# Adding the squares of two features on VectorE before the ones matmul that sums over features

## The chip, the core and the metric

The kernel runs on one core of a Trainium2 chip. TensorE (PE) does matmuls, VectorE (DVE) and ScalarE (ACT) elementwise work, GpSimd (POOL) some of it, SyncE (SP) issues the transfers of weights. Each engine runs its own instructions in order and waits for others by semaphores. The metric is device microseconds (us) of one execution.

## The reference

The program is a first transformer block (sliding-window attention, a recurrence, block attention, a feed-forward part) and then two layers of a second block, for 256 tokens with 1024 features. The change touches only the second block. Each of its layers has four stages, and each stage ends in a projection whose result is normalised before it is added to x:

```python
for l in range(DEPTH_2):                 # 2 layers
    h = rms_norm_2(x, ng[0])
    x = x + 0.5 * rms_norm_2(swiglu(h, w1, w3, w2), ng[1])      # feed-forward
    y = mixer_block(rms_norm_2(x, ng[2]), ...)                  # ends in merged @ w_out
    x = x + rms_norm_2(y, ng[3])
    y = cross_attention(rms_norm_2(x, ng[4]), ...)              # ends in o @ wo
    x = x + rms_norm_2(y, ng[5])
    x = x + 0.5 * rms_norm_2(swiglu(rms_norm_2(x, ng[6]), ...), ng[7])

def rms_norm_2(x, g):
    y = x * rsqrt(mean(x * x, axis=-1) + RMS_EPS)
    return y * g
```

The mean of x * x runs over the 1024 features. All is f32.

## The kernel before, in words

**Layout.** Features lie on the 128 partitions, in eight feature tiles (f = 0 to 7), and tokens on the free axis, so a feature tile is 128x256. A sum over features is therefore a sum over partitions and over the eight tiles: TensorE does it with a 128x128 matrix of ones, which adds up a tile and leaves the sum on every partition, and the eight tiles accumulate in one PSUM region (STAT, a part of misc_ps).

**Matmuls.** Weights come from memory in units of up to four k tiles by 256 columns (SP). ScalarE rounds a unit to weights_hi (`hi`, L1099), VectorE takes the rest weights_lo = weights - weights_hi (`lo`, L1421), and TensorE does three fp32r matmuls for each tile (L842). There are four buffers of split weights: at the step of unit m, ScalarE and VectorE split unit m + 3 (AHEAD = 3). The rounding of unit m + 3 waits until unit m - 1 has been multiplied, which frees its buffer. A GEMM over 256 output columns (two feature tiles, a pair) has six units in w2 of the feed-forward stages (22 k tiles: five units of four and one of two), and two units in the output projections of the mixer and of the cross-attention.

**Order.** `plan` writes one list of steps, and each engine runs through that list and does its own part of every step, in that order. For VectorE the step of unit m is the split of unit m + 3.

**The end of a stage.** Four GEMMs c = 0 to 3 give the four pairs of y. For each pair ScalarE writes the squares of two feature tiles to SQ (squares, L1181) and then y times the gain (L1184). Step `ystat` (L917) sums a pair's squares on TensorE: two fp32 matmuls by ones (L922). An fp32 matmul stands in the trace as two instructions, so a pair is four of them. The `ystat` of pair c - 1 stands behind GEMM c in the list, that of pair 3 follows that of pair 2:

```python
for c in range(4):
    gemm("w2", c * COLS, 22, ("HID", key), "evac_y", ft=2 * c, sq=s, yk=key, ...)
    if c:
        add("ystat", s=s, c=c - 1)
add("ystat", s=s, c=3)
add("rstd", key=key + "y", s=s, out="RY")
```

Then ScalarE takes the logarithm (L1103) and the exponential (L1105) of the sum, each with a load of its table before it, and VectorE multiplies y by the result (L1574) and adds it to x (L1576). In the mixer stage more lies in between: behind GEMM 1 the memory is transposed (L1062) and copied (L1903), behind GEMM 2 it is split (L1555) and squared, and after the `ystat` of pair 3 its own statistic is summed (L913), into the same PSUM region, once the logarithm has read it.

There are eight such stages (four feed-forward, two mixer, two cross-attention), so 32 `ystat` steps.

Of the kernel before, what the change touches and what calls it, by code (L numbers as in the profile page):

```python
# [19 lines left out]
ALU = mybir.AluOpType  # L20
# [4 lines left out]
T = 256  # L25
TT = T // P
D = 1024
NF = D // P
# [527 lines left out]
def build(nc, a, out, scratch, marks, final, stop=None):  # L556
# [10 lines left out]
    SQ = sb("squares", [P, NF, T])  # L567
# [8 lines left out]
    ONES, IDENT, FLIP, HEADS = (sb(n, [P, P]) for n in ("ones", "ident", "flip", "headsum"))  # L576
# [48 lines left out]
    STAT = PB[:, 3, :]  # L625
# [9 lines left out]
    sems = {n: ctx.enter_context(nc.semaphore(n)) for n in names}  # L635
# [4 lines left out]
    def up(name, reached=None, by=1):  # L640

        count[name] = count.get(name, 0) + by
        if reached is not None:
            marks[reached] = (name, count[name])
        return count[name]
# [4 lines left out]
    def at(*reached):  # L650

        assert reached in marks or not final, reached
        return marks.get(reached, (None, 1))[1]
# [161 lines left out]
    def _(pe):  # L815
        state = dict(att=None, scores=None)

        def stat_free(s):
            if stat_before.get(s) is not None:
                pe.wait_ge(*done(("stat_read", stat_before[s])))  # L820
# [96 lines left out]
        def pe_ystat(k):  # L917
            if k["c"] == 0:
                stat_free(k["s"])
            pe.wait_ge(sems["act_drain"], at("sqy", k["s"], k["c"]))  # L920
            for f in (2 * k["c"], 2 * k["c"] + 1):
                mm = pe.matmul(STAT[:, 0:T], ONES[:], SQ[:, f, :], start=f == 0, stop=f == NF - 1)  # L922
            mm.then_inc(sems["pe_norm"], 1)
            up("pe_norm", ("stat", k["s"]) if k["c"] == 3 else None)

# [141 lines left out]
        def pe_finish(k):  # L1067
# [3 lines left out]
            for t in range(TT):  # L1071
                for f in range(NF):
                    mm = pe.transpose(GPF[:, t * D + f * P:t * D + (f + 1) * P], X[:, f, t * P:(t + 1) * P], IDENT[:])
            mm.then_inc(sems["pe_setup"], 1)
            up("pe_setup", ("out_ps",))

        parts = dict(unit=pe_unit, params=pe_params, turn_x=pe_turn_x, mod=pe_mod, mod_col=pe_mod_col, bias=pe_bias, stat=pe_stat, ystat=pe_ystat,
                     rstd_cols=pe_rstd_cols, qk_norm=pe_qk_norm, scores=pe_scores, turn=pe_turn, pv=pe_pv,
                     subln=pe_subln, rnn_gate=pe_rnn_gate, cln_mean=pe_cln_mean, cln_var=pe_cln_var,
# [334 lines left out]
    def _(dve):  # L1414
# [147 lines left out]
        def vec_residual(k):  # L1562
# [14 lines left out]
                                     op0=ALU.mult, op1=ALU.add).then_inc(sems["vec_norm"], 1)  # L1577
            up("vec_norm", ("x", k["v"], p))

        def vec_rstd_cols(k):  # L1580
            dve.wait_ge(sems["pe_norm"], at("rt_ps", k["s"]))
            dve.tensor_copy(RT[:], STAT.rearrange("p (t q) -> p t q", q=P)[:, 0:TT, 0]).then_inc(sems["vec_norm"], 1)
            dve.wait_ge(sems["vec_norm"], up("vec_norm", ("stat_read", k["s"])))
# [316 lines left out]
        def vec_mem_turn(k):  # L1900
            for half in range(2):
# [2 lines left out]
                up("vec_norm", ("memf", f"l{k['l']}", half))  # L1904

        parts = dict(setup=vec_setup, params=vec_params, turn_x=vec_turn_x, mod=vec_mod, mod_sum=vec_mod_sum, adapt=vec_adapt, split=vec_split,
                     residual=vec_residual, rstd_cols=vec_rstd_cols, evac_qk=vec_evac_qk, qk_norm=vec_qk_norm,
                     evac_scaled=vec_scaled, evac_v2=vec_v2, softmax=vec_softmax, pv=vec_pv, subln=vec_subln,
                     pads1=vec_pads1, pads_f1=vec_pads_f1, rnn_conv=vec_rnn_conv, rnn_in=vec_rnn_in, rnn_mult=vec_rnn_mult, evac_yr=vec_evac_yr, gelu=vec_gelu, conv31=vec_conv31, rnn_scan=vec_rnn_scan,
                     evac_gate=vec_evac_gate, evac_branch=vec_evac_branch, evac_ffn_gate=vec_ffn_gate,  # L1910
# [167 lines left out]
```

## Time and profile before

| what | us |
|---|---|
| median of 3 runs | 2551.26 (2547.99 to 2553.19) |
| the profiled execution | 2549.33 |
| its span, first to last instruction | 2547.5 |
| busy: PE / DVE / ACT / POOL | 2365.3 / 1721.2 / 1323.8 / 387.5 |
| share of the chain that ended last: PE / DVE / ACT | 75% / 15% / 6% |

Busy time is the time in which an engine executes something; the chain of waits shows which of it the end depended on. Matmuls overlap: a record of 0.28 us is followed by the next after about 0.12 us, so paces are read from the chain or from start to start.

### The profile page before, as it was taken

The page shows a single profiled execution, that of the slowest core. Times are in us where ns is not written, and L with a number is a line of the kernel's source. Part 1 is how long each engine was busy: PE and PEld are TensorE (multiplying, and loading weights), DVE is VectorE, ACT ScalarE, POOL GpSimd, SP SyncE. Part 2 cuts the span into 40 slices and gives each one's busy share as a digit, 9 for nine tenths or more (in the row PEclk, how much of TensorE's full clock was granted, in tenths as well). Part 3 has the DMA queues.
Part 4 walks back from the last instruction along what each step waited for, and adds up shares of the span by engine and source line. Part 5 has one row for each costly group of instructions (what it writes and reads, how often), then busy time and mean ns, then how long its engine had stood idle before and what let it go on. Part 6 is the DMA issues. An engine that isn't in the chain of part 4 may idle for free.

```text
span 2547.5 us, 44221 instructions
## 1 busy us (share of the span) xinstructions
PE 2365.3 (93%) x18041; PEld 2265.1 (89%) x18041; DVE 1721.2 (68%) x2425; ACT 1323.8 (52%) x2074; POOL 387.5 (15%) x354
## 2 busy tenths in 40 slices
PE   6998998999998998999898998999998999898997
PEld 5976898999998997889898998998987889898997
DVE  5666886886664897887555654664897887555663
ACT  2565445664444654665635445444654765635443
POOL 1000000110110564530000110110464530000110
PEclk9998999999999998999999999999998999999998
DMA  8534584566655462446344654655462345344652
GB/s 246 161 108 141 169 252 140 184 193 211 187 179 158 147 185 83 124 133 195 120 133 125 183 183 140 182 173 175 133 199 75 120 135 182 132 139 120 184 175 82
DMA packets 402041, 400.41 MB, mean 157 GB/s; under 512 B 18006, under 2 KB 399304, under 8 KB 401841
## 3 DMA queue, kind: packets, MB, share of 16 engines
q1 hardware_dynamic: 399457, 389.27, 50.2%
q0 software_dynamic: 2384, 8.32, 1.2%
q8 instruction: 144, 2.36, 0.4%
q14 instruction: 56, 0.46, 0.1%
HBM read 396.45 MB, written 1.09 MB: 156 GB/s over the span
## 4 chain that ended last, share of the span: by engine, by line
PE 75%; DVE 15%; ACT 6%; issue 4%; DMA 1%; ACTq 0%; POOL 0%; DVEq 0%; POOLq 0%
PE gemm_ps L842 62%; DVE weights_lo L1421 4%; PE gemm_ps L845 3%; DVE y L1857 3%; PE misc_ps L970 2%; PE misc_ps L969 2%; PE misc_ps L913 2%; ACT L1103 1%; ACT weights_hi L1099 1%; DVE y L1574 1%; DVE x_res L1576 1%; DVE mod_partial L1518 1%; ACT h_hi L1170 1%; PE misc_ps L1002 1%; ACT e L1218 1%
## 5 line engine op out<-in xcount | busy, mean ns | idle before, releaser
L1421 DVE TENSOR_TENSOR weights_lo<-raw_weights,weights_hi 128x1024 fp32r<-128x1024 f32 x704 | 859.2, 1230 | 467.0 <-ACT weights_hi L1099 463.5
L842 PE MATMUL gemm_ps<-h_hi,weights_hi 128*128 128x256 f32 x3664 | 1068.0, 291 | 68.1 <-DVE h_lo L1555 45.4
L1099 ACT CAST weights_hi<-raw_weights 128x1024 fp32r<-128x1024 f32 x704 | 718.6, 1031 | 664.2 <-PE gemm_ps L842 612.0
L842 PE MATMUL gemm_ps<-h_lo,weights_hi 128*128 128x256 f32 x3664 | 1049.0, 286 | 0.0
L842 PE MATMUL gemm_ps<-h_hi,weights_lo 128*128 128x256 f32 x3664 | 1048.6, 286 | 0.0
L842 PEld LDWEIGHTS gemm_ps<-h_hi,weights_hi 128*128 128x128 f32 x3664 | 716.2, 195 | 81.5 <-issue 68.0
L842 PEld LDWEIGHTS gemm_ps<-h_lo,weights_hi 128*128 128x128 f32 x3664 | 716.7, 196 | 4.0 <-issue 3.0
L842 PEld LDWEIGHTS gemm_ps<-h_hi,weights_lo 128*128 128x128 f32 x3664 | 715.5, 195 | 0.0
L1986 POOL TENSOR_TENSOR y<-y,prod 128x256 f32<-128x256 f32 x240 | 249.3, 1039 | 352.4 <-ACT prod L1359 197.0
L1974 POOL TENSOR_TENSOR hidl<-hf,hidh 128x512 fp32r<-128x512 f32 x55 | 73.4, 1334 | 1291.1 <-ACT hidh L1343 1291.1
L842 PE MATMUL gemm_ps<-hidh,weights_hi 128*128 128x256 f32 x880 | 248.0, 282 | 0.3 <-DVE weights_lo L1421 0.3
L842 PE MATMUL gemm_ps<-hidh,weights_lo 128*128 128x256 f32 x880 | 245.4, 279 | 0.0
L842 PE MATMUL gemm_ps<-hidl,weights_hi 128*128 128x256 f32 x880 | 245.4, 279 | 0.0
L1857 DVE SCALAR_TENSOR_TENSOR y<-zp,param_cols,y 128x256 f32<-128x256 f32 x240 | 187.2, 780 | 5.7
L842 PE MATMUL gemm_ps<-gh,weights_hi 128*128 128x256 f32 x544 | 160.9, 296 | 18.4 <-DVE gl L1558 14.7
L842 PEld LDWEIGHTS gemm_ps<-hidh,weights_hi 128*128 128x128 f32 x880 | 165.2, 188 | 0.7 <-DVE weights_lo L1421 0.5
L842 PEld LDWEIGHTS gemm_ps<-hidh,weights_lo 128*128 128x128 f32 x880 | 165.4, 188 | 0.0
L842 PEld LDWEIGHTS gemm_ps<-hidl,weights_hi 128*128 128x128 f32 x880 | 164.7, 187 | 0.2
L842 PE MATMUL gemm_ps<-gl,weights_hi 128*128 128x256 f32 x544 | 154.7, 284 | 0.0
L842 PE MATMUL gemm_ps<-gh,weights_lo 128*128 128x256 f32 x544 | 154.4, 284 | 0.0
L842 PEld LDWEIGHTS gemm_ps<-gh,weights_hi 128*128 128x128 f32 x544 | 105.3, 194 | 22.1 <-issue 20.3
L1359 ACT ACTIVATE prod<-zp,param_cols 128x256 f32<-128x256 f32 x240 | 104.8, 505 | 3.2 <-POOL y L1986 3.2
(282 smaller groups left out, 2833.2 us busy)
## 6 DMA issues: line engine op xcount, KB each, us to landing
raw_weights<-in_ffn_w_dram SPq DMA_DIRECT2D x256, 512.0 KB, 3.8
raw_weights<-in_w_in_dram SPq DMA_DIRECT2D x200, 512.0 KB, 3.7
raw_weights<-in_w_mod_dram SPq DMA_DIRECT2D x48, 512.0 KB, 4.9
raw_weights<-in_w_up_dram SPq DMA_DIRECT2D x44, 512.0 KB, 4.5
raw_weights<-in_xattn_kv_dram SPq DMA_DIRECT2D x32, 512.0 KB, 3.8
raw_weights<-in_w_out_dram SPq DMA_DIRECT2D x24, 512.0 KB, 3.9
raw_weights<-in_w_down_dram SPq DMA_DIRECT2D x20, 512.0 KB, 4.7
raw_weights<-in_w_branch_dram SPq DMA_DIRECT2D x16, 512.0 KB, 4.4
```

Of the source, the lines that this page charges most:

```text
L842: mm = pe.matmul(ps[:, c, 0:T], w[:, m, kt, c * P:(c + 1) * P], x[:, f, :], start=start, stop=stop_)
L845: mm = pe.matmul(ps[:, c, 0:u["cols"]], x[:, f, c * P:(c + 1) * P], w[:, m, kt, 0:u["cols"]], start=start, stop=stop_)
L913: mm = pe.matmul(STAT[:, 0:T], ONES[:], squares[:, f, :], start=f == 0, stop=f == NF - 1)
L969: pe.matmul(ps, c["q"][m][:, qt * P:(qt + 1) * P], c["k"][m][:, 0:nk], start=True, stop=False)
L970: mm = pe.matmul(ps, FLIP[:], c["hank"][:, c["head"][m], T - nk:T], start=False, stop=True)
L1002: mm = pe.matmul(PV[:, f * T:(f + 1) * T], c["v"][f][kb], PT[:, kb * T:(kb + 1) * T], start=kb == 0, stop=kb == 1)
L1099: act.copy(WH[s], RAWB[:, u["raw"] % RAW, 0:u["nkt"], 0:u["cols"]]).then_inc(sems["weights_rounded"], 1)
L1359: act.activation(o_m["prod"][:, b, i, :], o_m["zp"][:, f, j:j + T], ACT.Copy, scale=col(f"dw{k['l']}", 8 * j + f)).then_inc(sems["act_prod ...
L1421: dve.tensor_tensor(WL[s], RAWB[:, u["raw"] % RAW, 0:u["nkt"], 0:u["cols"]], WH[s], ALU.subtract).then_inc(sems["weights_rest"], 1)
L1857: dve.scalar_tensor_tensor(out=Y[:, f, :], in0=o_m["zp"][:, f, j:j + T], scalar=col(f"dw{l}", 8 * j + f), in1=Y[:, f, :], op0=ALU.mult, op ...
L1974: pool.tensor_tensor(l_[:, s, :], src, h[:, s, :], ALU.subtract).then_inc(sems["hidden_rest"], 1)
L1986: pool.tensor_tensor(Y[:, f, :], Y[:, f, :], o_m["prod"][:, b, i, :], ALU.add).then_inc(sems["pool_conv"], 1)
```

## The change

The `ystat` step gets a part on VectorE: it waits for ScalarE's squares of the pair and adds the second feature tile to the first, in place. TensorE waits for that addition in place of the squares and does one ones matmul instead of two. Nothing else is edited.

```diff
         def pe_ystat(k):
             if k["c"] == 0:
                 stat_free(k["s"])
-            pe.wait_ge(sems["act_drain"], at("sqy", k["s"], k["c"]))
-            for f in (2 * k["c"], 2 * k["c"] + 1):
-                mm = pe.matmul(STAT[:, 0:T], ONES[:], SQ[:, f, :], start=f == 0, stop=f == NF - 1)
+            pe.wait_ge(sems["vec_norm"], at("sqy_sum", k["s"], k["c"]))
+            mm = pe.matmul(STAT[:, 0:T], ONES[:], SQ[:, 2 * k["c"], :], start=k["c"] == 0, stop=k["c"] == 3)
             mm.then_inc(sems["pe_norm"], 1)
             up("pe_norm", ("stat", k["s"]) if k["c"] == 3 else None)
...
+        def vec_ystat(k):
+            f = 2 * k["c"]
+            dve.wait_ge(sems["act_drain"], at("sqy", k["s"], k["c"]))
+            dve.tensor_tensor(SQ[:, f, :], SQ[:, f, :], SQ[:, f + 1, :], ALU.add).then_inc(sems["vec_norm"], 1)
+            up("vec_norm", ("sqy_sum", k["s"], k["c"]))
...
-                     residual=vec_residual, rstd_cols=vec_rstd_cols, evac_qk=vec_evac_qk, qk_norm=vec_qk_norm,
+                     residual=vec_residual, ystat=vec_ystat, rstd_cols=vec_rstd_cols, evac_qk=vec_evac_qk, qk_norm=vec_qk_norm,
```

VectorE's order at the end of the first feed-forward stage before, from the splits of w2's first units on (L1421 is the split of a unit, L1574 the first instruction of the residual; a unit of two k tiles is 128x512):

```order
532 L1421 TENSOR_TENSOR weights_lo<-raw_weights,weights_hi 128x512
533 L1421 TENSOR_TENSOR weights_lo<-raw_weights,weights_hi 128x1024 x5
534 L1421 TENSOR_TENSOR weights_lo<-raw_weights,weights_hi 128x512
535 L1421 TENSOR_TENSOR weights_lo<-raw_weights,weights_hi 128x1024 x5
536 L1421 TENSOR_TENSOR weights_lo<-raw_weights,weights_hi 128x512
537 L1421 TENSOR_TENSOR weights_lo<-raw_weights,weights_hi 128x1024 x5
538 L1421 TENSOR_TENSOR weights_lo<-raw_weights,weights_hi 128x512
539 L1421 TENSOR_TENSOR weights_lo<-raw_weights,weights_hi 128x1024 x3
540 L1574 TENSOR_TENSOR y<-y,rstd_y 128x512
```

And the same place in the changed kernel, where the addition is L1582 and the split L1420:

```order
532 L1420 TENSOR_TENSOR weights_lo<-raw_weights,weights_hi 128x512
533 L1420 TENSOR_TENSOR weights_lo<-raw_weights,weights_hi 128x1024 x5
534 L1420 TENSOR_TENSOR weights_lo<-raw_weights,weights_hi 128x512
535 L1420 TENSOR_TENSOR weights_lo<-raw_weights,weights_hi 128x1024 x3
536 L1582 TENSOR_TENSOR squares<-squares 128x256
537 L1420 TENSOR_TENSOR weights_lo<-raw_weights,weights_hi 128x1024 x2
538 L1420 TENSOR_TENSOR weights_lo<-raw_weights,weights_hi 128x512
539 L1420 TENSOR_TENSOR weights_lo<-raw_weights,weights_hi 128x1024 x3
540 L1582 TENSOR_TENSOR squares<-squares 128x256
541 L1420 TENSOR_TENSOR weights_lo<-raw_weights,weights_hi 128x1024 x2
542 L1420 TENSOR_TENSOR weights_lo<-raw_weights,weights_hi 128x512
543 L1420 TENSOR_TENSOR weights_lo<-raw_weights,weights_hi 128x1024 x3
```

The addition of pair c - 1 stands behind the split of the third unit of GEMM c + 1, three units ahead of the unit that TensorE multiplies last before it comes to the same step. The additions of pairs 2 and 3 follow behind row 543.

At the end of the mixer stage VectorE has this in the changed kernel (ml is the lower part of the split memory, memf its copy):

```order
821 L1420 TENSOR_TENSOR weights_lo<-raw_weights,weights_hi 128x1024 x4
822 L1582 TENSOR_TENSOR squares<-squares 128x256
823 L1908 COPY memf<-misc_ps 128x1024 x2
824 L1420 TENSOR_TENSOR weights_lo<-raw_weights,weights_hi 128x1024 x2
825 L1582 TENSOR_TENSOR squares<-squares 128x256
826 L1554 SCALAR_TENSOR_TENSOR ml<-memf,param_cols,mh 128x256 x8
827 L1420 TENSOR_TENSOR weights_lo<-raw_weights,weights_hi 128x1024 x2
828 L1582 TENSOR_TENSOR squares<-squares 128x256 x2
829 L1573 TENSOR_TENSOR y<-y,rstd_y 128x512
```

Before, the same rows stand there without the three rows of L1582: the last two additions come behind eight parts of the memory's split and two weight splits.

On TensorE nothing changes its place; one ones matmul is left of two. Before, behind GEMM 1 of the first feed-forward stage:

```order
5086 L842 MATMUL gemm_ps<-hidh,weights_lo 128x256
5087 L922 MATMUL misc_ps<-squares,ones 128x256 x2
5088 L842 MATMUL gemm_ps<-hidh,weights_hi 128x256
```

## Rows read from the trace of the kernel before

**Rows 1.** The page, busy time, share of the span and instructions.
```profile
PE 2365.3 (93%) x18041; PEld 2265.1 (89%) x18041; DVE 1721.2 (68%) x2425; ACT 1323.8 (52%) x2074; POOL 387.5 (15%) x354
```

**Rows 2.** Chain of waits, 778 to 836 us: start, length, engine, line.
```profile
781.57 0.86 PE misc_ps L922 x4
782.43 15.55 PE gemm_ps L842 x132
797.98 0.86 PE misc_ps L922 x4
798.84 15.56 PE gemm_ps L842 x132
...
829.73 0.50 DVE h_lo L1555
830.22 0.04 issue
```

**Rows 3.** Timeline, 795 to 801 us: start, length, engine, instruction [idle before].
```profile
797.70 0.74 PEld L922 LDWEIGHTS misc_ps<-squares,ones 128*128 128x128 f32 x4
797.74 1.22 DVE L1421 TENSOR_TENSOR weights_lo<-raw_weights,weights_hi 128x1024 fp32r<-128x1024 f32 x1 [1.60 <-ACT weights_hi L1099]
797.82 1.03 PE L922 MATMUL misc_ps<-squares,ones 128*128 128x256 f32 x4
```

**Rows 4.** Groups of instructions by form: count, busy us, mean ns, idle before.
```profile
L1555 DVE SCALAR_TENSOR_TENSOR h_lo<-pu,h_hi 128x256 fp32r<-128x256 f32 x16 | 5.5, 417 | 0.0
...
L1738 DVE TENSOR_TENSOR xc<-xc,s_all 128x256 f32<-128x256 f32 x8 | 3.4, 425 | 0.3
```

**Rows 5.** Timeline, projections of a mixer and a cross stage.
```profile
1199.94 2.77 DVE L1555 SCALAR_TENSOR_TENSOR h_lo<-pu,h_hi 128x256 fp32r<-128x256 f32 x8
...
1210.54 1.22 DVE L1421 TENSOR_TENSOR weights_lo<-raw_weights,weights_hi 128x1024 fp32r<-128x1024 f32 x1 [0.49 <-ACT weights_hi L1099]
...
1211.97 0.74 PEld L922 LDWEIGHTS misc_ps<-squares,ones 128*128 128x128 f32 x4
...
1346.16 1.23 DVE L1421 TENSOR_TENSOR weights_lo<-raw_weights,weights_hi 128x1024 fp32r<-128x1024 f32 x1 [0.49 <-ACT weights_hi L1099]
...
1347.59 0.74 PEld L922 LDWEIGHTS misc_ps<-squares,ones 128*128 128x128 f32 x4
```

**Rows 6.** Chain of waits behind the mixer's third projection.
```profile
1222.18 0.60 ACT squares L1181
```

**Rows 7.** Timeline, the end of a feed-forward stage.
```profile
814.15 1.23 DVE L1421 TENSOR_TENSOR weights_lo<-raw_weights,weights_hi 128x1024 fp32r<-128x1024 f32 x1 [1.60 <-ACT weights_hi L1099]
...
815.77 1.28 ACT L1103 ACT_TABLE_LOAD   x1
817.07 0.47 ACT L1103 ACTIVATE rstd_y<-misc_ps,eps 128x256 f32<-128x256 f32 x1
```

**Rows 8.** Timeline, the ends of a mixer and a cross stage.
```profile
1229.75 2.36 DVE L1421 TENSOR_TENSOR weights_lo<-raw_weights,weights_hi 128x1024 fp32r<-128x1024 f32 x2 [2.53 <-ACT weights_hi L1099]
...
1233.19 0.47 ACT L1103 ACTIVATE rstd_y<-misc_ps,eps 128x256 f32<-128x256 f32 x1
...
1233.72 5.41 PE L913 MATMUL misc_ps<-msq,ones 128*128 128x256 f32 x16 [1.38 <-ACT rstd_y L1103]
...
1361.14 0.60 ACT L1181 ACTIVATE squares<-gemm_ps 128x512 f32<-128x512 f32 x1 [1.78 <-PE gemm_ps L842]
...
1363.78 0.47 ACT L1103 ACTIVATE rstd_y<-misc_ps,eps 128x256 f32<-128x256 f32 x1
```

**Rows 9.** Timeline of TensorE, two matmuls behind idle time.
```profile
145.28 1.22 PE L939 MATMUL misc_ps<-small_squares,headsum 128*128 128x512 f32 x1 [1.54 <-ACT rg L1272]
...
1200.50 0.36 PE L842 MATMUL gemm_ps<-h_hi,weights_hi 128*128 128x256 f32 x1 [1.94 <-DVE h_lo L1555]
```

**Rows 10.** Busy by stretch: PE, PEld, DVE, ACT, POOL, granted clock, DMA share, GB/s.
```profile
145.00:146.00 1.00, 0.71 (x1) 0.50 (x2) 0.00 (x0) 1.00 (x2) 0.00 (x0) 0.62 0.85 251
1200.00:1201.00 1.00, 0.50 (x4) 0.53 (x5) 1.00 (x5) 0.94 (x3) 0.00 (x0) 1.00 0.97 325
```

## The prediction

> **What bounds the kernel now.** I read the page first: TensorE (PE) is busy 93% of the span [rows 1]. Which instruction on it matters is not in that share, so the second view was the chain of waits around one output projection of a feed-forward stage [rows 2]. The reader is to see there 132 matmuls of a projection (15.55 us), 0.86 us of L922 (the ones matmuls of the change), and again 132 matmuls: nothing but TensorE, back to back, and L922 stands on the path as itself. An ones matmul is recorded as two instructions, so four of them for a pair of features cost 0.86 us, or 0.43 us a matmul. The third view was the timeline around one such place, for what VectorE (DVE) does at that moment [rows 3]. The fourth was the same for the ends of stages, where TensorE waits for others [rows 7, 8].
>
> **Where the 32 places are.** Eight stages (four feed-forward, two mixer, two cross-attention) have four output projections c = 0 to 3 each. The program puts the sum of pair c-1 behind projection c, and the sums of pairs 2 and 3 both behind projection 3. So per stage two sums stand between projections (pairs 0 and 1) and two at its end. 64 ones matmuls become 32.
>
> **What is removed.** One matmul of 0.43 us in each place. Of the 32, the 16 between projections can be on the path; the 16 at the ends stand beside ScalarE's (ACT) evacuation and table load.
>
> **What is added, feed-forward stages.** Each sum now waits for an addition on VectorE, and VectorE runs in program order. The order listing shows what is ahead of the addition: the split of weights (L1421) for the third unit after the one that TensorE is in. Why that is late: the split waits for ScalarE's rounding, and that waits for the end of TensorE's unit before. In w2 a projection has 22 k tiles, five units of four and a last one of two. The last is 12 of 132 matmuls, 15.55 x 12 / 132 = 1.41 us; the split takes 1.22 [rows 3] and the rounding comes before it. In the rows [rows 3]: TensorE starts L922 at 797.70 (its weight load), VectorE begins the split only at 797.74 and ends it at 798.96. Then comes the addition. 128x256 f32 TENSOR_TENSOR takes 0.425 us (L1738) [rows 4]. Consecutive VectorE instructions with no dependence overlap a little: eight of 0.417 us [rows 4] took 2.77 us [rows 5], one each 0.34 us, so a record overlaps the one before by about 0.08. The addition ends at 798.96 - 0.08 + 0.42 = 799.30. From a VectorE end to TensorE: the chain has h_lo, 0.04 us of issue and then a matmul [rows 2]; I take 0.05. TensorE starts the sum at 799.35 instead of 797.70: +1.65 us; one matmul less: -0.43; net +1.22. With the overlap left out it is +1.30; I take 1.25 for all eight places (four stages, pairs 0 and 1), whose chain pieces repeat: 8 x 1.25 = **+10.0 us**. Nothing gives that back: VectorE and ScalarE get ahead by the same time, but in that stretch they wait for TensorE (the split's own row has 1.60 us of waiting before it [rows 3]), and the next projection is 15.55 us of TensorE again. Behind the addition on VectorE waits the next split, which waits for ScalarE anyway as this one does, so it is not later.
>
> **Mixer and cross stages.** Here a projection is two full units of 24 matmuls, so split and unit end together. Mixer: VectorE ends its split at 1210.54 + 1.22 = 1211.76, TensorE loads for L922 at 1211.97 [rows 5]. Addition to 1212.10, release 1212.15: +0.18 - 0.43 = -0.25. Cross: 1346.16 + 1.23 = 1347.39, to 1347.73, release 1347.78 against 1347.59: +0.19 - 0.43 = -0.24 [rows 5]. The mixer's pair 1 counts nothing: behind it the chain leaves TensorE for ScalarE at 1222.18 [rows 6] and stays there until the end of the stage. That leaves pair 0 in two mixers and both pairs in two cross stages: 6 x -0.24 = **-1.4 us**.
>
> **Ends of stages.** Feed-forward: VectorE's split ends at 814.15 + 1.23 = 815.38, two additions to 815.72 and 816.06, TensorE from 815.77, both sums in the 0.12 + 1.03 us that four such instructions take from the first weight load [rows 3], so until 816.92. The logarithm of L1103 starts at 817.07, held by a table load that began at 815.77 and takes 1.28 us [rows 7]. Cost nothing, with 0.15 us to spare; if that cover were gone it would be up to 0.7 us in each. Cross: squares end at 1361.74, addition to 1362.2, sum to about 1363.0, logarithm at 1363.78 [rows 8]: nothing. Mixer: VectorE is late with two splits, 1229.75 + 2.36 = 1232.11 [rows 8]; additions to 1232.45 and 1232.79, TensorE 1232.50 to 1233.65, logarithm at 1233.69 instead of 1233.19: +0.50 us. The statistic of the memory (L913) waits for that read at 1233.72, so it is on the path. Two mixers: **+1.0 us**.
>
> **Sum.** +10.0 - 1.4 + 1.0 = +9.6 us. The profiled execution took 2549.33 us (span 2547.5), so 2558.9 by its own time. It lies 1.9 us under the median of the runs, 2551.26; from the median it is 2560.9. I say 2561.
>
> **What the trace doesn't show.** An idle gap of about 1.65 us inside dense matmuls, eight times. For the granted clock after it there are rows on both sides [rows 9, 10]: after 1.94 us of idle time at 1200.50 the stretch has clock 1.00 (2.4 GHz); after 1.54 us at 145.28 the clock was 0.62 in that microsecond, part of it at 1.2 GHz. What a fall costs: L913 took 5.41 us for 16 instructions at 1233.72 [rows 8] where 4 take 0.86 [rows 2], that is 3.44, so 1.97 us lost. Bounds for eight gaps: 0 and 8 x 1.97 = 15.8 us. I take 0, since the longer of the two gaps, which like these lies before feature matmuls of a projection, kept its clock, and keep the other end for the range. The addition itself is bounded by 0.34 us (the overlapped pace) and 0.425 without overlap: at most 0.1 us a place, 1 us in all.
>
> **A rule to weigh.** The profile's busiest engine is TensorE, and it loses work in this change [rows 1]. The Trainium skill ("Perfetto Trace Analysis", Identifying the Most-Contended Engine) says to optimise the engine with the highest occupancy first, though it warns that matmul busy time misleads. By that rule the change is a gain, 16 x 0.43 = 6.9 us on the path. The trace speaks against it: what counts is who releases the sum, and that becomes the split and the addition.
>
> **Rivals.**
> 1. Forecast, stalls at the feed-forward projections: +9.6, 2561, own range 2557 to 2564. 67%.
> 2. The clock falls in a part of the gaps, two to eight of them at 1.5 to 2 us: 2564 to 2576. For it: the row at 145.28, and the gap of 1.38 us before L913. Against it: the row at 1200.50. 16%.
> 3. The other side, faster: the sums are released in time and only the removed matmuls count, -6.9 us, 2544. Its place is the same as mine, pairs 0 and 1 between projections; it decides if the addition ends before TensorE has finished its unit, 1.65 us earlier than I work out. For it: chain row L922 and 0.43 us each [rows 2]. Against it: the order of the splits. 4%.
> 4. Stalls are there but absorbed, within 5 us of before: if the units behind waited for something else than TensorE. Against it: the chain holds TensorE alone [rows 2]. About 2553. 9%.
> 5. The ends cost too (feed-forward ends, 0.15 us of cover): three or four more times 0.3 to 0.7 us: 2563. 4%.
>
> This kernel can tell 0.2% (5.1 us) from no change. Faster by more: 5% (case 3 and a little of 4). Within: 11%. Slower: 84%. The range 2555 to 2570 leaves out case 3, half of case 4 and the worst of case 2.
>
> **What would show it.** In the profile after: VectorE has 32 new instructions of about 0.42 us; the first two of each feed-forward stage start as a split ends. TensorE is idle about 1.6 us before the sum there, eight times, released by VectorE. In cross stages the gap is 0.2 us. Ones matmuls of the sums: 64 instructions in place of 128. The stretch from one projection to the next in feed-forward stages goes from 16.41 us (15.55 + 0.86) to about 17.66. Granted clock 1.00 across these gaps confirms case 1 over 2. The forecast is wrong if the gaps are absent, or present with no longer span.

## The result: 11.5 us slower, and the profile after

| | before | after |
|---|---|---|
| median (6 runs each) | 2552.23 us (2547.89 to 2557.76) | 2563.75 us (2562.29 to 2564.89) |
| ratio, 95% interval | | 1.0045 [1.0031, 1.0059] |
| profiled execution / its span | 2549.33 / 2547.5 us | 2563.45 / 2561.6 us |
| granted clock, mean | 0.966 | 0.958 |

The forecast was 2561 us, +9.6. The page after, busy time, answers to [rows 1]:

```profile
PE 2357.3 (92%) x17977; PEld 2256.9 (88%) x17977; DVE 1732.2 (68%) x2457; ACT 1323.9 (52%) x2074; POOL 388.3 (15%) x354
```

TensorE has 64 instructions and 8 us of work less, VectorE 32 instructions and 11 us more, and the whole takes longer. Where, the chain of waits around the first feed-forward stage says (start, length, engine, line; the split is L1420 now, the ones matmul L921, the addition L1582; PEld below is TensorE's loading of weights). It answers to [rows 2]:

```profile
780.93 1.06 ACT weights_hi L1098
...
782.02 1.23 DVE weights_lo L1420
...
783.24 0.34 DVE squares L1582
783.59 0.14 issue
783.72 0.67 PE misc_ps L921 x2
784.39 15.56 PE gemm_ps L842 x132
...
801.32 0.70 PE misc_ps L921 x2
802.02 15.57 PE gemm_ps L842 x132
```

Before, this stretch held TensorE alone. Now, at the first place, it leaves TensorE for a rounding on ScalarE, the split on VectorE and the addition behind it. (At the second place the view follows ScalarE's evacuation instead; see below.) From one projection's first matmul to the next one's it is 802.02 - 784.39 = 17.63 us; before it was 16.41, and 17.66 was forecast. The timeline at the second of these places (idle time before an instruction in brackets) answers to [rows 3]:

```profile
799.70 1.23 DVE L1420 TENSOR_TENSOR weights_lo<-raw_weights,weights_hi 128x1024 fp32r<-128x1024 f32 x1 [1.60 <-ACT weights_hi L1098]
...
800.85 0.42 DVE L1582 TENSOR_TENSOR squares<-squares 128x256 f32<-128x256 f32 x1
...
801.32 0.30 PEld L921 LDWEIGHTS misc_ps<-squares,ones 128*128 128x128 f32 x2 [1.58 <-DVE squares L1582]
801.32 0.70 PE L921 MATMUL misc_ps<-squares,ones 128*128 128x256 f32 x2 [1.38 <-ACT y L1183]
```

The addition begins 1.15 us behind the start of the split, overlapping its end by 0.08, and TensorE begins 0.05 us after the addition's end. The weight load waited 1.58 us. (For the matmul the view names ScalarE's evacuation, y, which ends within 0.04 us of the addition. The program has TensorE wait for the addition alone, and in e5 below the ones matmul at the first place starts at 783.48 while y runs until 783.71. So y is not what it waits for.)

The ends of stages, answering to [rows 7, 8], are these in the timeline: feed-forward, mixer, and the last ones matmul of a cross stage.

```profile
818.48 0.75 DVE L1582 TENSOR_TENSOR squares<-squares 128x256 f32<-128x256 f32 x2
818.95 0.73 PEld L921 LDWEIGHTS misc_ps<-squares,ones 128*128 128x128 f32 x4 [1.58 <-DVE squares L1582]
818.95 1.13 PE L921 MATMUL misc_ps<-squares,ones 128*128 128x256 f32 x4 [1.38 <-DVE squares L1582]
818.95 1.28 ACT L1102 ACT_TABLE_LOAD   x1
820.25 0.47 ACT L1102 ACTIVATE rstd_y<-misc_ps,eps 128x256 f32<-128x256 f32 x1
...
1235.14 2.36 DVE L1420 TENSOR_TENSOR weights_lo<-raw_weights,weights_hi 128x1024 fp32r<-128x1024 f32 x2 [2.53 <-ACT weights_hi L1098]
...
1237.41 0.75 DVE L1582 TENSOR_TENSOR squares<-squares 128x256 f32<-128x256 f32 x2
...
1237.89 1.13 PE L921 MATMUL misc_ps<-squares,ones 128*128 128x256 f32 x4 [3.99 <-DVE squares L1582]
1239.06 0.47 ACT L1102 ACTIVATE rstd_y<-misc_ps,eps 128x256 f32<-128x256 f32 x1 [0.49 <-PE misc_ps L921]
...
1366.76 0.70 PE L921 MATMUL misc_ps<-squares,ones 128*128 128x256 f32 x2 [0.54 <-DVE squares L1582]
```

In the feed-forward stage the sums end at 820.08 and the logarithm starts at 820.25, when its table is loaded: hidden, as forecast. In the mixer stage the logarithm waits 0.49 us for the sum: the +0.50 of the forecast, at this instruction. Whether it reaches the end of the kernel is another matter, and is taken up at the end.

**How the stages are compared.** ScalarE's squares of a stage's four pairs are four marks on each trace. From the first to the fourth lie projections 1 to 3 and the sums of pairs 0 and 1, nothing else. Before, in the first feed-forward stage: 766.05 to 814.43, 48.38 us; after, 766.74 to 817.61, 50.87: +2.49, for two places. From the fourth mark to the logarithm is the stage's end. This is what each kernel shows against before (mean of its stages, us; "sum" is all eight stages and the mixer ends; the last column is the ratio of its runs to runs of the kernel before taken beside them on the same chip. The chips differ between experiments, so the ratios compare, not the medians):

| kernel | feed-forward (x4) | mixer (x2) | cross (x2) | mixer end (x2) | sum | ratio [interval] |
|---|---|---|---|---|---|---|
| after | +2.49 | -0.20 | -0.47 | +0.48 | +9.6 | 1.0045 [1.0031, 1.0059] |
| e2 | +2.48 | 0 | 0 | 0 | +9.9 | 1.0037 [1.0024, 1.0051] |
| e3 | 0 | -0.20 | -0.47 | +1.42 | +1.5 | 0.9995 [0.9987, 1.0004] |
| e4 | +3.34 | 0 | 0 | 0 | +13.4 | 1.0050 [1.0037, 1.0063] |
| e5 | +1.87 | -0.43 | -0.87 | +1.15 | +7.2 | 1.0032 [1.0020, 1.0043] |
| e6 | -0.88 | -0.43 | -0.87 | 0 | -6.1 | 0.9983 [0.9974, 0.9992] |
| e1 | -0.88 | -0.44 | -0.87 | +0.91 | -4.3 | 0.9988 [0.9979, 0.9996] |
| e7 | -0.88 | -0.44 | -0.87 | +0.56 | -5.0 | 0.9988 [0.9977, 0.9998] |
| e8 | -1.74 | -0.86 | -1.71 | +2.36 | -7.4 | 0.9983 [0.9974, 0.9993] |
| e9 | +7.30 | -0.20 | -0.47 | +1.42 | +30.7 | 1.0133 [1.0119, 1.0147] |
| e10 | -1.74 | -0.51 | -1.71 | +0.07 | -11.3 | 0.9964 [0.9950, 0.9978] |

0.001 of the ratio is 2.5 us. Several of these kernels compute something else than the program (their expectations say what they leave out or count twice); they are there for their time alone.

In the cuts of code, what stands behind a `#` is a note.

### The profile page after: what moved, and what is told of

Its sections match the earlier page's. It is cut to its first block, busy times and chain, and to the rows that moved or that the text cites. A ratio compares the mean times of both kernels' runs of the same rounds, so it can differ in the third digit from the quotient of the medians.

```text
span 2561.6 us, 44125 instructions
## 1 busy us (share of the span) xinstructions
PE 2357.3 (92%) x17977; PEld 2256.9 (88%) x17977; DVE 1732.2 (68%) x2457; ACT 1323.9 (52%) x2074; POOL 388.3 (15%) x354
## 3 DMA queue, kind: packets, MB, share of 16 engines
q8 instruction: 144, 2.36, 0.4%
## 4 chain that ended last, share of the span: by engine, by line
PE 75%; DVE 15%; ACT 6%; issue 3%; DMA 1%; ACTq 0%; POOL 0%; DVEq 0%; POOLq 0%
PE gemm_ps L842 62%; DVE weights_lo L1420 4%; PE gemm_ps L845 3%; DVE y L1862 3%; PE misc_ps L969 2%; PE misc_ps L968 2%; PE misc_ps L913 2%; ACT weights_hi L1098 1%; DVE y L1573 1%; ACT L1102 1%; DVE x_res L1575 1%; DVE mod_partial L1517 1%; ACT h_hi L1169 1%; PE misc_ps L1001 1%; ACT e L1217 1%
## 5 line engine op out<-in xcount | busy, mean ns | idle before, releaser
L1420 DVE TENSOR_TENSOR weights_lo<-raw_weights,weights_hi 128x1024 fp32r<-128x1024 f32 x704 | 859.5, 1231 | 474.6 <-ACT weights_hi L1098 470.8
L842 PEld LDWEIGHTS gemm_ps<-gl,weights_hi 128*128 128x128 f32 x544 | 106.0, 195 | 1.2 <-issue 1.0
```

What stands on the lines that cost most here:

```text
L842: mm = pe.matmul(ps[:, c, 0:T], w[:, m, kt, c * P:(c + 1) * P], x[:, f, :], start=start, stop=stop_)
L1420: dve.tensor_tensor(WL[s], RAWB[:, u["raw"] % RAW, 0:u["nkt"], 0:u["cols"]], WH[s], ALU.subtract).then_inc(sems["weights_rest"], 1)
```

## The experiments

### e2 and e3: the two halves of the change

In e2 only the feed-forward places of pairs 0 and 1 have the addition, all others two matmuls as before; e3 is the complement.

```diff
+def FOLD(k):
+    return k.get("ffn", False) and k["c"] < 2      # e3: not (...)
...
+            if FOLD(k):
                 pe.wait_ge(sems["vec_norm"], at("sqy_sum", k["s"], k["c"]))
                 mm = pe.matmul(STAT[:, 0:T], ONES[:], SQ[:, 2 * k["c"], :], ...)
+            else:
+                pe.wait_ge(sems["act_drain"], at("sqy", k["s"], k["c"]))
+                for f in (2 * k["c"], 2 * k["c"] + 1):
...
         def vec_ystat(k):
+            if not FOLD(k):
+                return
```

> The change is made only for pairs 0 and 1 of the four feed-forward stages (8 of 32 places); elsewhere the sum is as before. My theory (the addition stands behind a late weight split, so TensorE waits about 1.6 us before each of these sums and saves 0.43): +1.2 us a place as the profile after shows, +9.6 to 10.0 us over before, ratio about 1.0038, which is nearly all of the change's cost. Rival 'the cost lies at the stage ends': within 2 us of before. Rival 'the clock falls after the gaps': more than +12 us, with granted clock under 1 in the stretch behind them.

> The complement: the change everywhere but in those 8 places. My theory: -1.4 us between the projections of the mixer and cross stages, +1.0 us at the two mixer ends, so -0.4 us, the same as before within the noise. Rival 'the cost lies at the stage ends': +5 to +10 us.

Measured: e2 2563.90 us, ratio 1.0037, that is 9.4 us with an interval of 6 to 13; e3 2551.01 us, ratio 0.9995. Eight places of 32 carry the cost; the other 24 together are within what can be told from nothing. The rows of e2 and e3 in the table are those of the changed kernel, split in two, but for one: the mixer end of e3 costs 1.42 instead of 0.48 us. Its timeline of TensorE (the ones matmul is L926 here, the sum of the memory's squares L917):

```profile
1231.34 2.08 PE L926 MATMUL misc_ps<-squares,ones 128*128 128x256 f32 x4 [4.00 <-DVE squares L1593]
1233.98 6.70 PE L917 MATMUL misc_ps<-msq,ones 128*128 128x256 f32 x16 [0.56 <-ACT rstd_y L1111]
```

The same four instructions took 1.13 us in the changed kernel, behind the same idle 3.99 us. The missing 0.95 us is the clock, not the wait. Windows over the four instructions, in e3 and in the changed kernel (the column before the last two is the granted clock):

```profile
1231.30:1233.40 2.10, 2.06 (x4) 1.18 (x4) 0.32 (x1) 0.71 (x1) 0.00 (x0) 0.50 0.89 261
...
1237.80:1239.00 1.20, 1.11 (x4) 0.67 (x4) 0.37 (x2) 0.76 (x1) 0.00 (x0) 0.98 0.96 313
```

### e6 and e5: no addition; then only the wait

e6 does one ones matmul for each pair with no addition (VectorE's part of the step is never called; the squares of the odd feature tiles are left out of the sum). e5 is e6 with TensorE waiting, for pairs 0 to 2, until the split ahead of which the addition would stand is done.

```diff
-            pe.wait_ge(sems["vec_norm"], at("sqy_sum", k["s"], k["c"]))
+            pe.wait_ge(sems["act_drain"], at("sqy", k["s"], k["c"]))
+            if k["c"] < 3 and state["m"] + AHEAD < len(splits):                     # e5 alone
+                pe.wait_ge(sems["weights_rest"], at("rest", state["m"] + AHEAD))    # e5 alone
             mm = pe.matmul(STAT[:, 0:T], ONES[:], SQ[:, 2 * k["c"], :], ...)
```

> One ones matmul a pair and no addition at all (the squares of the odd feature tiles are left out of the sum), TensorE waits for ScalarE's squares as before. This bounds what the removed matmuls can be worth. My theory: only those between projections on the path count, 14 x 0.43 = -6.0 us against before. Rival 'every TensorE instruction removed shortens the run, since it is the busiest engine': 32 x 0.43 = -13.8 us.

> One ones matmul a pair, no addition; for pairs 0, 1 and 2 TensorE waits for the weight split behind which the addition stood (the squares of the odd feature tiles are left out). It parts the wait into split and addition. My theory: the split alone makes 1.31 us of the delay in a feed-forward place, net +0.88, 8 x 0.88 = +7.0; in mixer and cross the split is done in time, 6 x -0.43 = -2.6; sum about +4.5 us over before. Rival 'the addition on VectorE is what costs': -6 us, like the run without an addition.

Measured: e6 2549.00 us, ratio 0.9983; e5 2557.55 us, ratio 1.0032. The chain of e6:

```profile
781.62 0.43 PE misc_ps L921 x2
782.05 15.54 PE gemm_ps L842 x132
797.60 0.43 PE misc_ps L921 x2
```

So a ones matmul on the path is worth 0.44 us (0.88 for two places), as forecast, and taking them away does make the kernel faster. In e5 the wait for the split alone turns -0.44 into +0.94 a place: 1.38 of the 1.68 us that the wait costs is the split; the rest, 1.24 - 0.94 = 0.30, is the addition. The expectation missed one thing, the mixer ends: they cost 1.15 us each, and with them the sum is +7.2, where the ratio stands for 8 and +4.5 was expected. TensorE waits there for two late splits, and its four instructions then run at half clock (granted clock 0.50 in 1236.70:1238.90):

```profile
1236.79 2.05 PE L924 MATMUL misc_ps<-squares,ones 128*128 128x256 f32 x4 [3.93 <-DVE weights_lo L1423]
```

Of the 1.15 us, 2.05 - 1.13 = 0.92 is the clock again.

### e4: the wait with nothing removed

Feed-forward places of pairs 0 and 1 only: the addition and the wait as in the change, and still two matmuls.

```diff
             if FOLD(k):
                 pe.wait_ge(sems["vec_norm"], at("sqy_sum", k["s"], k["c"]))
-                mm = pe.matmul(STAT[:, 0:T], ONES[:], SQ[:, 2 * k["c"], :], ...)
+                for f in (2 * k["c"], 2 * k["c"] + 1):
+                    mm = pe.matmul(STAT[:, 0:T], ONES[:], SQ[:, f, :], ...)
```

> Only in pairs 0 and 1 of the feed-forward stages: TensorE waits for VectorE's addition, but still does both ones matmuls (the sum then counts one feature tile twice). The price of the wait alone. My theory: 8 x 1.65 = +13.2 us over before, 0.43 us a place more than the run with one matmul there. Rival 'the matmul saved is worth nothing, since TensorE idles there anyway': the same time as with one matmul, +9.6 us.

Measured: 2562.67 us, ratio 1.0050. 3.34 us for two places is 1.67 for one; the prediction's bare wait was 1.65. It and the matmul add up: 1.67 - 0.44 = 1.23, the changed kernel has 1.24.

### e1: the addition ahead of the split

The addition of pairs 0 to 2 is issued on VectorE just ahead of the split behind which it stood; all else is as in the change.

```diff
+        early, last = {}, None
+        for i, (kind, k) in enumerate(steps):
+            if kind == "unit":
+                last = i
+            elif kind == "ystat" and k["c"] < 3:
+                early[last] = k
+        for i, (kind, k) in enumerate(steps):
+            if i in early:
+                vec_ystat(early[i])
...
-            if kind in parts:
+            if kind in parts and not (kind == "ystat" and k["c"] < 3):
```

> The change with one move: on VectorE the addition of pairs 0, 1 and 2 stands ahead of the split that is issued with the last unit of the next projection, not behind it. My theory: it is then done long before TensorE comes to the sum, the waits are gone and the removed matmul counts: 14 places x -0.43 = -6.0 us, and +0.9 us at the two mixer ends, so about -5 us against before (2547) and -16 us against the change. Rival 'it is the addition or its semaphore as such, not its place': no better than the change, about +10 us.

Measured: 2547.77 us, ratio 0.9988. The same 32 additions and the same matmuls, one place earlier on one engine, and the feed-forward stages go from +2.49 to -0.88, the same as with no addition at all. The mixer ends cost 0.91 us each where 0.9 was expected for both together; the clock makes half of it (granted 0.50 in 1232:1236, where two instructions of L921 took 1.22 us; in e7, at full clock, 0.70). The timeline:

```profile
796.30 0.42 DVE L1582 TENSOR_TENSOR squares<-squares 128x256 f32<-128x256 f32 x1
...
797.95 0.30 PEld L921 LDWEIGHTS misc_ps<-squares,ones 128*128 128x128 f32 x2
797.99 1.23 DVE L1420 TENSOR_TENSOR weights_lo<-raw_weights,weights_hi 128x1024 fp32r<-128x1024 f32 x1 [1.27 <-ACT weights_hi L1098]
```

The addition is done 1.23 us before TensorE loads the ones.

### e7: the addition on GpSimd

```diff
-            dve.wait_ge(sems["act_drain"], at("sqy", k["s"], k["c"]))
-            dve.tensor_tensor(SQ[:, f, :], SQ[:, f, :], SQ[:, f + 1, :], ALU.add).then_inc(sems["vec_norm"], 1)
+            pool.wait_ge(sems["act_drain"], at("sqy", k["s"], k["c"]))
+            pool.tensor_tensor(SQ[:, f, :], SQ[:, f, :], SQ[:, f + 1, :], ALU.add).then_inc(sems["pool_sum"], 1)
```

> The changed kernel with all 32 additions on GpSimd in place of VectorE (a semaphore of their own, the ones matmul waits for it). Theory (the cost in the feed-forward places is that VectorE's addition stands behind the split that waits for ScalarE's rounding, not the addition itself): GpSimd has nothing in its queue there, so the addition starts when the squares are written; it takes some 1 us on GpSimd (its 128x256 additions take 1042 ns each in the trace of before), which still ends before the last matmuls of the next projection. All places then gain what one matmul is worth: in-stage growth like the kernel without an addition, feed-forward -0.88, mixer -0.43, cross -0.87 a stage, ratio about 0.998; at the stage ends the slower addition may cost 0.6 in each of the eight, so 0.998 to 1.000. Rival (the addition itself or its semaphore is what costs, on whatever engine): feed-forward +2 or more a stage, ratio 1.004.

Measured: 2546.92 us, ratio 0.9988. The additions take a median of 857 ns there, twice VectorE's, and cost nothing between the projections: the feed-forward stages show -0.88 again. The rival, that the addition or its semaphore is what costs on whatever engine, falls. Timeline:

```profile
797.24 0.87 POOL L2022 TENSOR_TENSOR squares<-squares 128x256 f32<-128x256 f32 x1 [15.11 <-ACT squares L1180]
```

### e9: a longer gap

Three more additions in a row in the eight feed-forward places, to see whether the clock falls behind a longer gap.

```diff
+            if k.get("ffn") and k["c"] < 2:
+                for i in range(3):
+                    dve.wait_ge(sems["vec_norm"], count["vec_norm"])
+                    dve.tensor_tensor(SQ[:, f, :], SQ[:, f, :], SQ[:, f + 1, :], ALU.add).then_inc(sems["vec_norm"], 1)
...
```

> The change with three further additions in series in each of the 8 feed-forward places (the pair's second tile is counted four times), so the gaps grow by 3 x 0.43 us to about 2.7 us. It tells whether the price of a gap is its length or also the clock behind it. My theory: linear, 8 x 1.3 = +10.4 us over the change, +22 over before, granted clock 1.00 behind the gaps. Rival 'the clock falls behind such gaps': up to 2 us more in each, +12 to +26 over the change, with matmul records of 0.41 us behind the gaps.

Measured: 2584.59 us, ratio 1.0133. The timeline of TensorE at the first two of the eight places and the next to last:

```profile
783.70 0.67 PE L921 MATMUL misc_ps<-squares,ones 128*128 128x256 f32 x2 [2.85 <-DVE squares L1587]
...
802.68 0.75 PE L921 MATMUL misc_ps<-squares,ones 128*128 128x256 f32 x2 [2.76 <-DVE squares L1587]
...
2520.61 1.19 PE L921 MATMUL misc_ps<-squares,ones 128*128 128x256 f32 x2 [2.85 <-DVE squares L1587]
```

And the two microseconds behind the first two (busy time of PE, PEld, DVE, ACT, POOL, then the granted clock):

```profile
784.40:786.40 2.00, 2.00 (x19) 2.00 (x18) 0.29 (x1) 0.00 (x0) 0.00 (x0) 1.00 0.34 95
803.50:805.50 2.00, 2.00 (x11) 2.00 (x11) 0.26 (x1) 0.00 (x0) 0.00 (x0) 0.50 0.36 99
```

Behind six of the eight gaps the clock is at 0.50 (1.2 GHz), behind two of 2.85 us it stays full. The theory of a linear price falls, and its rival holds. The three additions cost 1.38 us at a place without a fall (17.69 us from one pair's squares to the next in the changed kernel, 19.06 here, at the first place of the first stage), so a stage would be 2.49 + 2 x 1.38 = +5.25; the four show +6.26, 6.72, 8.24 and 7.97 with one, one, two and two falls. A fall cost 1.0 to 1.5 us. The eight gaps of the changed kernel, 1.38 to 1.47 us on TensorE's matmuls, all kept the clock. Two of the eight windows:

```profile
785.80:787.80 2.00, 2.00 (x20) 2.00 (x19) 0.01 (x1) 0.49 (x1) 0.00 (x0) 1.00 0.45 151
803.50:805.50 2.00, 2.00 (x19) 2.00 (x18) 0.00 (x0) 0.56 (x1) 0.00 (x0) 1.00 0.51 148
```

### e8 and e10: towards a faster kernel

If a sum between projections can be had for nothing, none is needed there. In e8 VectorE adds each pair into pair 0 (128x512), ahead of the split as in e1, and TensorE does two ones matmuls at the stage's end.

```diff
         def pe_ystat(k):
+            if k["c"] < 3:
+                return
+            stat_free(k["s"])
+            pe.wait_ge(sems["vec_norm"], at("sqy_sum", k["s"], 3))
+            for f in (0, 1):
+                mm = pe.matmul(STAT[:, 0:T], ONES[:], SQ[:, f, :], start=f == 0, stop=f == 1)
...
         def vec_ystat(k):
...
+            s = slice(2 * k["c"], 2 * k["c"] + 2)
...
+            dve.tensor_tensor(SQ[:, 0:2, :], SQ[:, 0:2, :], SQ[:, s, :], ALU.add).then_inc(sems["vec_norm"], 1)
```

> VectorE adds the squares of pairs 1, 2 and 3 into pair 0 (three additions of 128x512 a stage, pairs 1 and 2 ahead of the split as in the run before), and TensorE does two ones matmuls a stage, at its end, in place of eight. My theory: nothing is left between projections, 14 places x -0.86 = -12.0 us against before, and at the ends two matmuls behind an addition of 0.69 us: nothing in feed-forward and cross, +0.8 us in the mixers (two): -10.4 us, 2541. Rival 'the longer addition at the end is exposed': 0.5 us or more in each of eight ends, -6 us.

Measured: 2547.88 us, ratio 0.9983, so 4.3 us faster where 10.4 was expected. Between projections it gains twice what e1 does (-1.74 a feed-forward stage), but each mixer end gives 2.36 us back, where 0.4 was expected (0.93 of it is the clock, as the last line below shows), and three of the four feed-forward ends 0.20. At the mixer end the chain shows why (e8; the addition is L1588):

```profile
1229.97 1.11 issue
1231.08 0.68 DVE squares L1588
1231.76 0.06 DVE weights_lo L1422
1231.82 0.99 issue
1232.81 0.69 DVE squares L1588
1233.51 0.14 issue
1233.64 2.06 PE misc_ps L923 x4
```

Two additions, each behind a split, are in series, and the four instructions behind them ran at the lowered clock (2.06 us, not 1.13). e10 takes both away: pairs 1 and 2 are added with the evacuation of their own projection, and pair 3 is not added but gets its own two matmuls.

```diff
+            pe.wait_ge(sems["vec_norm"], at("sqy_sum", k["s"], 2))
+            for f in (0, 1):
+                pe.matmul(STAT[:, 0:T], ONES[:], SQ[:, f, :], start=f == 0, stop=False)
+            pe.wait_ge(sems["act_drain"], at("sqy", k["s"], 3))
+            for f in (6, 7):
+                mm = pe.matmul(STAT[:, 0:T], ONES[:], SQ[:, f, :], start=False, stop=f == 7)
...
+            if kind == "evac_y" and k["sq"] is not None and k["ft"] in (2, 4):
+                vec_ystat(dict(s=k["sq"], c=k["ft"] // 2))
```

> A version meant to be faster: VectorE adds pair 1 and pair 2 into pair 0 (two additions of 128x512 a stage), each issued with the evacuation of its own projection and so ahead of the next splits; pair 3 is not added. TensorE does four ones matmuls at the end of a stage (two of the accumulated pair, two of pair 3), none between the projections. Theory: between the projections two whole gaps of matmuls go, in-stage -1.74 feed-forward, -0.86 mixer, -1.71 cross as in the kernel that accumulates all four pairs, sum -12.1; the ends stand as before (that kernel gave 3.0 back at each mixer end, where its last two additions stood behind splits, and some 1.2 at each feed-forward end). So about -9 to -12, ratio 0.9955 to 0.9965. Rival (what a stage end or a memory transfer behind it gives back is given back whatever the cause): ratio 0.998 as in the kernel that accumulates four.

Measured: 2540.03 us, ratio 0.9964 [0.9950, 0.9978], 5.6 to 12.7 us faster than before. The expected range was met, with two shifts inside it: a mixer stage gains 0.50 us and not 0.86, since the first addition (0.69 us) now stands ahead of the memory's copy on the chain, and the first mixer end still costs 0.12 us, the second nothing. Chain of waits of e10 up to the end of the first feed-forward stage:

```profile
772.95 38.41 PE gemm_ps L842 x326
811.36 0.02 issue
811.38 0.60 ACT squares L1185
```

Where the chain of before had projections with ones matmuls between them [rows 2], and that of after had five pieces on three engines, 326 matmuls now follow one another.

### e11: the changed kernel a second time

> The changed kernel again, unaltered, for a second profile. Theory (the 2.4 to 2.9 us that its first profile shows from the last squares of two feed-forward stages to the mixer stage behind, in stretches that the change doesn't touch, come with the place at which the granted clock falls, not with the change): in-stage growth again +2.48 a feed-forward stage, -0.20 mixer, -0.47 cross to within 0.05, but the stretches between the stages differ from the first profile by up to 3 us, and stretches of lowered clock stand at other places. Rival (the change has a further cost there): the same +2.4 and +2.9 again.

Measured, one execution: 2561.86 us, span 2560.1. The stages show +2.48, -0.20 and -0.47 again. From the last squares of the first feed-forward stage to the first of the mixer stage it is +1.79 us against before, +2.41 in the first profile; at the same stretch of layer 2 it is +2.89 and +2.90. Two profiles of one kernel decide little: one number repeats and one does not.

The other kernels say more. None edits that stretch, and in them it differs from before by -1.6 to +3.4 us: -1.24 and +2.79 within e10 alone, +0.30 and -1.61 in e4, +1.85 and +3.43 in e6, which has no added wait at all. So these microseconds come and go without the change. What they go with is the granted clock. In layer 2 the stretch takes 389.4 us at a mean granted clock of 0.969 (e4), 391.0 at 0.965 (before, e3), 390.6 at 0.961 (e1, e5, e7), 391.9 and 392.8 at 0.956 and 0.957 (e9, e2), 393.8 to 393.9 at 0.952 (both profiles of the changed kernel, e8, e10) and 394.5 at 0.944 (e6). Layer 1 has nearly the same order (390.9 us at 0.965, 394.5 and 394.8 at 0.948), with e5 off it by 2 us. Why one profile has more stretches of lowered clock there than another stays open.

## Why the prediction was right, step by step

**Who releases the sum.** Forecast: the split, then the addition. The chain after has just these at the first place, and at the second the weight load names the addition. e1 and e7 take the addition from behind the split in two ways and both reach e6's number to 0.01 us.

**Feed-forward places, 8 x 1.25.** Measured 1.24. The parts: bare wait 1.67 (e4; forecast 1.65), matmul 0.44 (e6; forecast 0.43), overlap of a VectorE record with the one before 0.08 (forecast 0.08). This came out because each part had a row; only the release at the first place of a stage took 0.14 us (783.58 to 783.72) where 0.05 was written, so that place is +1.28 and the second +1.21.

**Mixer and cross, 6 x -0.24.** Measured -0.20 a mixer stage (one place) and -0.47 a cross stage (two): -1.3 in all against -1.4.

**Ends.** Forecast +0.50 at a mixer end, 0 elsewhere; measured +0.48 at the logarithm, and 0.00 at the six others (2.64 us from squares to logarithm in both kernels). Rival 5 is out. But the forecast also took these 2 x 0.5 us to reach the end of the kernel, and that is not shown. From the last squares of a mixer stage to the first of the cross stage it was 111.60 us in both layers before; it is 111.18 and 111.59 after, 111.56 and 111.77 in the second profile, all at a mean granted clock of 0.969. What offsets the later logarithm is open. In the first layer the statistic of the memory (L913) ran almost wholly at the lowered clock (6.77 us, 5.41 before), and a later part of the stretch at the full clock: before, the next four L913 instructions took 2.05 us on the chain, after 1.13. Where the clock falls moves more here than the 0.48 us in question.

**Clock.** Forecast: no fall in the eight gaps. None fell. e9 shows that the rival was real and its size about right: 1.0 to 1.5 us a fall where 1.5 to 2 was written. Here luck has a part: the forecast took the side of one of two rows that spoke against each other, and neither told why it should hold; with gaps of 2.8 us that choice would have missed 8.2 us (what the four stages of e9 show beyond 5.25 each).

**The sum.** +9.6 against a measured ratio that stands for 8 to 15 us, and against +14.1 in the two profiled spans. The stages with the mixer ends hold 9.6 of the 14.1, 8.6 of it between the first and the fourth squares of stages; 5.3 lie in the two unedited stretches of e11's section, +0.7 ahead of the first stage, and -1.5 in the rest, nearly all of it directly behind the two mixer ends, as just told. So what is shown part by part is the 8.6 between projections. That the whole came within 3 us of the forecast owes something to parts that it did not have and that happened to be small in sum. The prediction compares two single executions as if unedited stretches were equal; they are so to about 3 us each. It had no term for that; the range covered it.

**A slip that changed nothing.** Rival 3 and the rule count 16 x 0.43 = 6.9 us as the most that the removed matmuls can give. By the forecast's own reading the mixer's pair 1 is not on the path, so it is 14 x 0.43 = 6.0; e6's stages show 6.1.

**The rule.** The Trainium skill ("Perfetto Trace Analysis", Identifying the Most-Contended Engine) says to optimise the engine with the highest occupancy first. Read as "work taken from it pays", which is the prediction's reading, it fails in this case: TensorE's busy time fell by 8 us and the kernel lost 11. e6 shows the condition under which it holds: the same work taken away with no new wait gains 4 us.

## What to carry to other kernels

Moving work from the busiest engine to one with time to spare pays only if the second engine gets to it in time. What decides is not its busy share (68%) but what stands ahead of the new instruction in its program order, and what that waits for. Here the same addition cost 10 us behind a split, and nothing between the projections ahead of it. At the mixer ends, where the last addition still stands behind two splits, it cost 0.9 us, half of it the clock. Once an off-path engine does such an addition ahead of its slow step, fold further: one sum at the end in place of four (e10). Where the last additions stand behind splits again, the end of the stage takes a part of it back (e8).

## What the runs showed of the hardware

The same idle time can be followed by either clock level. Ahead of the mixer's projections TensorE was idle 1.94 us in the kernel before and kept the full clock [rows 9, 10]; in the changed kernel the same place shows matmuls of 0.42 us behind 1.93 us idle. Timeline and window:

```profile
1204.59 0.36 PE L842 MATMUL gemm_ps<-h_hi,weights_hi 128*128 128x256 f32 x1 [1.93 <-DVE h_lo L1554]
...
1204.95 0.42 PE L842 MATMUL gemm_ps<-h_hi,weights_lo 128*128 128x256 f32 x1
```

```profile
1204.00:1210.00 6.00, 5.41 (x33) 5.44 (x34) 3.92 (x10) 2.37 (x4) 0.76 (x1) 0.72 0.37 98
```

A gap's length alone doesn't tell, then. Nor does it tell when the fall comes: behind an idle time of 3.99 us the four ones matmuls of the changed kernel still ran at full clock (1.13 us) and the clock fell as they ended, so that L913 behind them took 6.77 us; in e3, with 4.00 us, it had fallen before they began (2.08 us). What does tell was not settled. The sixteen instructions of L913 at a mixer end took 5.41 us at both ends before, 6.77 and 5.17 after, and 5.15 and 6.58 in the second profile of the same kernel: one place, one program, 1.6 us apart.
